# Attention gate in seven-product pairs, with the gated outputs' low parts on GpSimd, in a hybrid decoder layer

## The chip, the cores and the metric

One core of a Trainium2 chip runs the whole layer in one launch. The metric is the device time of that launch in microseconds (us). A change of about 0.2% (2.2 us) is what a measurement of this kernel can tell from none.

## The reference

`x` is 1 x 1024 x 1024 in fp32. Cut to what matters here:

```python
h = rmsnorm(x, ln_pre)
c_val, c_glu, c_gate, q, k, v, a_gate, g_conv, g_attn = split_columns(h @ w_in)
u  = c_val * sigmoid(c_glu)
c  = causal_depthwise_conv(u, w_dw, 31 taps) + b_dw
ya = silu(layernorm(c, ln_g, ln_b)) @ w_pw
ya = (ya * silu(c_gate)) @ w_br_conv
yb = sliding_window_attention(q, k, v, sinks)       # 16 query heads, 2 K/V heads, window 128
yb = (yb * silu(a_gate)) @ w_br_attn
m  = sigmoid(g_conv) * ya + sigmoid(g_attn) * yb
x  = x + rmsnorm(m @ w_out, ln_post)
x  = x + sigmoid(x @ w_ple_gate) * (p @ w_ple_proj)
```

`h @ w_in` makes, among others, the 1024 columns of `a_gate`, which this change is about.

## The kernel before

Activations lie channels by tokens: 8 tiles (KT) of 128 channels, 1024 tokens in two halves of 512. Every fp32 product is made of three TensorE passes in the fp32r format: each operand is split into a high part (ScalarE rounds it) and a low part (raw minus high, on VectorE or GpSimd), and hi*hi, lo*hi, hi*lo are added in PSUM. A matmul has 128 rows, 128 columns and 512 tokens.

Two kinds of product occur. A **plain tile** makes one tile of 128 output channels: 8 k-tiles x 3 passes x 2 halves = 48 matmuls (`tile`, `pairs`, `product`, L757). A **seven-product pair** makes two output tiles i and i+4 by Strassen-Winograd's scheme on 2 x 2 blocks: seven products of 4 k-tiles x 3 passes = 12 matmuls, 84 together instead of 96 (`early_product`, L944). It needs sums of weight blocks (`early_sum`, GpSimd, L1259), high and low parts of seven weight blocks (ScalarE L1437, GpSimd L1243, a ring of six slots in `pair_w`), copies of three products (`early_keep`, ScalarE L1451), and two subtractions (`early_take`, VectorE L2136).

The program's stages in order:

1. Start: `p @ w_ple_proj`, norm of x, two plain tiles each of GLU and value.
2. **Early stage**: the list `EARLY` has 18 pairs s = 0 to 17: GLU, value and conv gate (10), queries (3), swish gate of the conv branch CGATE (4), K/V (1, the last). Products run in `ORDER` P1, Q5, P6, P2, P7, Q3, P4. ScalarE prepares the high part of product b+6 behind the events of product b (`early_high`, `early_events`). VectorE runs the 31-tap convolution here, in `taps` between the products; the last of its eight rows ends in pair 17. GpSimd adds six finished rows into `sums` (`add_to_mean`), for the LayerNorm's mean.
3. Two plain query tiles (Q0), with K, V and rotary work beside them.
4. **Attention**: 16 steps p (8 blocks of 128 queries x 2 K/V groups). In each, TensorE makes `scores(p)`, `outputs(p-2)`, `turn(p-1)` (transposed probabilities) and 24 matmuls of a plain gate tile of g_attn (L1093). VectorE does `maxima`, `with_sinks`, `mask_turned(p-1)`, every second step one weight low part (`tile_low`), and `normalise`. ScalarE does `gate_half`, `copy_outputs`, `copy_turned`, the exponentials (`exps`) and weight high parts. GpSimd adds the last two rows into `sums`, then issues 16 DMAs of weight sums for later stages, each waiting for the one ahead of it (L1331, L1333).
5. **D0**: 8 plain tiles of a_gate. While they run, attention's last outputs are made, `conv_mean` and `wide_sums` (eight matmuls by `ones`) sum the statistics over channels, ScalarE applies silu to the gate, VectorE multiplies it into the attention outputs `qo`, both split the product (`split_high`, `split_low` into `o_hi`, `o_lo`), and VectorE and ScalarE make the LayerNorm statistics (`centre`, `square_conv`, `add_to_variance`, `root_step`, up to the semaphore `ln_root`).
6. **E0**: 8 plain tiles of `w_br_attn` on `o_hi`, `o_lo`, with scaling, silu and splitting of the convolution's rows beside them.
7. The two conv-branch products in seven-product pairs, then `w_out` and `w_ple_gate` in plain tiles.

The order on each engine is the order of the code; semaphores alone hold engines together. PSUM tensor `psg` holds the products in banks, `psb` the convolution's accumulators, then scores, then sums over channels.

## Time and profile before

| | us |
|---|---|
| median of 3 runs (1099.11 to 1099.71) | 1099.31 |
| the profiled execution's own time | 1099.16 |
| its span | 1097.4 |
| TensorE busy | 1090.2 (99%) |
| VectorE / ScalarE / GpSimd busy | 853.8 / 479.6 / 315.4 |
| attention, 441.7 to 583.8 | 142.1 |
| D0 with attention's end, 583.8 to 677.0 | 93.2 |
| E0, 677.0 to 764.0 | 87.0 |

Positions are us from the span's start. The chain of work that ended last is TensorE for 92% of the span; L757 and L944 have 33% and 30%. A matmul's duration (389 ns) contains its pipeline; what a further matmul costs is the distance between starts. VectorE's busy share by slices is 9 tenths over most of the early stage and 6 to 9 in attention; GpSimd's is 7 to 9 in the early stage, 5 and 2 in the two slices after it, and 0 beyond.

### The profile page before, as it was taken

The numbers are of one execution on the slowest core, as the hardware profiler recorded it, in microseconds if no ns is written. First come the engines' busy times: TensorE is split into PE (matmuls) and PEld (weight loads), VectorE is DVE, ScalarE is ACT, GpSimd is POOL, SyncE is SP. The second block draws the span as 40 slices with busy tenths as digits, with TensorE's granted clock in tenths as the row PEclk, the third lists the DMA queues.
The fourth block names the chain that finished last, engine by engine and source line by source line (L and its number), as shares of the span: only waits on it lengthen the run. The fifth ranks groups of instructions, "written<-read, shape, count | busy, mean of one in ns | idle before, by whom it ended". The sixth has DMA issues, their size and how long they took to land.

```text
span 1097.4 us, 16190 instructions
## 1 busy us (share of the span) xinstructions
PE 1090.2 (99%) x5992; PEld 886.1 (81%) x5992; DVE 853.8 (78%) x1201; ACT 479.6 (44%) x914; POOL 315.4 (29%) x252
## 2 busy tenths in 40 slices
PE   9999999999999999999999999999999999999998
PEld 7888888888888887777777888888888888888887
DVE  5998989989998986888874876466668778366776
ACT  6643343443334432665664433334436426344332
POOL 1069888887779852200000000000000000000000
PEclk9999999999999999999999999999999999999999
DMA  9802231422233348567751112354644843334655
GB/s 347 353 1 79 77 116 43 153 77 77 87 134 116 116 152 239 155 177 209 193 156 58 58 39 77 115 202 144 194 142 152 298 153 103 98 127 134 202 181 191
DMA packets 52822, 157.01 MB, mean 143 GB/s; under 512 B 6296, under 2 KB 7064, under 8 KB 50424
## 3 DMA queue, kind: packets, MB, share of 16 engines
q1 hardware_dynamic: 37232, 96.44, 25.8%
q10 hardware_dynamic: 13216, 42.87, 11.4%
q0 software_dynamic: 2304, 16.78, 6.2%
q8 instruction: 43, 0.70, 0.2%
q14 instruction: 27, 0.22, 0.1%
HBM read 124.90 MB, written 47.02 MB: 157 GB/s over the span
## 4 chain that ended last, share of the span: by engine, by line
PE 92%; DVE 3%; DMA 2%; ACT 1%; issue 1%; SPq 1%; POOL 0%; ACTq 0%; DVEq 0%
PE psg L757 33%; PE psg L944 30%; PE psb L1185 11%; PE psg L1093 7%; PE psg L781 2%; PE psb L1007 1%; PE psg L1064 1%; PE psg L1185 1%; DMA x_rows<-x_rows 1%; PE psg L810 1%; PE psg L1138 1%; PE psg L1025 1%; PE psg L1059 1%; ACT probs L1569 1%; DMA pack<-rotary 1%
## 5 line engine op out<-in xcount | busy, mean ns | idle before, releaser
L1243 POOL TENSOR_TENSOR pair_w<-early_raw,pair_w 128x512 fp32r<-128x512 f32 x117 | 157.5, 1356 | 79.4 <-ACT pair_w L1437 79.3
L944 PE MATMUL psg<-early_hi,pair_w 128*128 128x512 f32 x576 | 177.6, 389 | 0.2
L2098 DVE SCALAR_TENSOR_TENSOR psb<-conv,cols,psb 128x510 f32<-128x510 f32 (+6 forms) x196 | 137.1, 739 | 0.0
L944 PE MATMUL psg<-h_hi,pair_w 128*128 128x512 f32 x432 | 133.1, 389 | 1.3 <-DVE ring L2136 1.3
L944 PEld LDWEIGHTS psg<-early_hi,pair_w 128*128 128x128 f32 x576 | 107.9, 188 | 23.6 <-issue 1.4
L1437 ACT ACTIVATE pair_w<-early_raw 128x512 fp32r<-128x512 f32 x117 | 71.1, 626 | 117.4 <-POOL early_raw L1259 84.8
L1226 POOL TENSOR_TENSOR rstd<-mean_sq,expo 128x4 f32<-128x4 f32 x3 | 3.1, 1022 | 382.7 <-DVE mean_sq L1901 363.5
L944 PE MATMUL psg<-early_lo,pair_w 128*128 128x512 f32 x288 | 112.0, 389 | 0.0
L1887 DVE TENSOR_TENSOR w_lo<-w_raw,w_hi 128x1024 fp32r<-128x1024 f32 x57 | 69.8, 1224 | 41.0 <-ACT w_hi L1350 35.7
L944 PEld LDWEIGHTS psg<-h_hi,pair_w 128*128 128x128 f32 x432 | 81.0, 188 | 18.4 <-issue 1.7
L2098 DVE SCALAR_TENSOR_TENSOR psb<-fir_sum,fir_taps,psb 128x511 f32<-128x511 f32 (+14 forms) x120 | 88.8, 740 | 0.0
L1350 ACT ACTIVATE w_hi<-w_raw 128x1024 fp32r<-128x1024 f32 x58 | 61.2, 1055 | 53.9 <-PE psg L757 49.0
L944 PE MATMUL psg<-h_lo,pair_w 128*128 128x512 f32 x216 | 84.0, 389 | 0.0
L1259 POOL TENSOR_TENSOR early_raw<-early_raw 128x512 f32<-128x512 f32 x54 | 72.8, 1348 | 4.2
L1185 PE MATMUL psb<-s_hi,pair_w 128*128 128x512 f32 x240 | 73.9, 389 | 0.0
L944 PEld LDWEIGHTS psg<-early_lo,pair_w 128*128 128x128 f32 x288 | 54.1, 188 | 11.3
L757 PE MATMUL psg<-h_hi,w_hi 128*128 128x512 f32 x192 | 59.6, 391 | 0.0
L757 PE MATMUL psg<-h_hi,w_lo 128*128 128x512 f32 x192 | 59.2, 389 | 0.0
L757 PE MATMUL psg<-h_lo,w_hi 128*128 128x512 f32 x192 | 59.1, 389 | 0.0
L1680 ACT ACTIVATE pair_w<-block_raw 128x512 fp32r<-128x512 f32 x56 | 34.5, 626 | 41.8 <-PE psb L1185 21.5
L1185 PEld LDWEIGHTS psb<-s_hi,pair_w 128*128 128x128 f32 x240 | 45.1, 188 | 9.4
L1093 PE MATMUL psg<-h_hi,w_hi 128*128 128x512 f32 x128 | 51.8, 405 | 0.0
(344 smaller groups left out, 2467.9 us busy)
## 6 DMA issues: line engine op xcount, KB each, us to landing
w_raw<-weights SPq DMA_DIRECT2D x60, 512.0 KB, 3.3
gates<-ring ACTq DMA_DIRECT2D x30, 512.0 KB, 3.2
w_sums<-w_pairs POOLq DMA_DIRECT2D x12, 1024.0 KB, 8.0
ring<-gates ACTq DMA_DIRECT2D x24, 512.0 KB, 4.0
early_raw<-w_pairs SPq DMA_DIRECT2D x9, 1024.0 KB, 5.3
block_raw<-w_sums SPq DMA_DIRECT2D x32, 256.0 KB, 2.7
early_raw<-w_pairs SPq DMA_DIRECT2D x9, 768.0 KB, 4.4
block_raw<-w_pairs SPq DMA_DIRECT2D x24, 256.0 KB, 3.2
```

Source lines behind the costliest of these rows:

```text
L757: mm = nc.tensor.matmul(psg[:, slot, h * HALF:(h + 1) * HALF], w[:, wslot, (wk + k) * P:(wk + k + 1) * P], r[:, k, h * HALF:(h + 1) * HALF ...
L781: mm = nc.tensor.matmul(psg[:, slot, h * HALF:(h + 1) * HALF], w[:, slot, k * P:(k + 1) * P], r[:, k, h * HALF:(h + 1) * HALF], start=(k = ...
L944: mm = nc.tensor.matmul(bank, pair_w[:, at_w, w, k * P:(k + 1) * P], r[:, k, :], start=(not onto and k == 0 and m == 0), stop=(k == KP - 1 ...
L1093: mm = nc.tensor.matmul(gate_bank(p), w[:, t % 2, k * P:(k + 1) * P], r[:, k, half], start=(k == 0 and m == 0), stop=(k == KT - 1 and m == 2))
L1185: mm = nc.tensor.matmul(bank, pair_w[:, at_w, w, k * P:(k + 1) * P], r[:, k, :], start=(not onto and k == 0 and m == 0), stop=(k == KP - 1 ...
L1243: nc.gpsimd.tensor_tensor(pair_w[:, at_w, 1, :], early_source(s, n), pair_w[:, at_w, 0, :].bitcast(F32), ALU.subtract).then_inc(early_spli ...
L1259: nc.gpsimd.tensor_tensor(early_block(s, out), early_block(s, a), early_block(s, b), ALU.add).then_inc(early_summed, 1)
L1350: nc.scalar.activation(w_hi[:, j % 2, :], w_raw[:, j % 2, :], ACT.Copy).then_inc(w_hi_ready, 1)
L1437: nc.scalar.activation(pair_w[:, early_slot(b), 0, :], early_source(s, n), ACT.Copy).then_inc(early_split_hi, 1)
L1680: nc.scalar.activation(pair_w[:, pair_slot(b), 0, :], block_raw[:, b % 7, :], ACT.Copy).then_inc(pair_hi, 1)
L1887: nc.vector.tensor_tensor(w_lo[:, slot, :], w_raw[:, slot, :], w_hi[:, slot, :].bitcast(F32), ALU.subtract).then_inc(w_lo_ready, 1)
L2098: own.step(stt(acc[:, shift:], source[:, 0:HALF - shift], weight, acc[:, shift:], ALU.mult, ALU.add))
```

## The change

- The four pairs of a_gate (`AGATE`, silu) enter `EARLY` between CGATE and K/V, which becomes pair 21. The D0 tiles are gone; E0 is now tile 14. AGATE's results are written to DRAM in rows of 128 tokens (`AGATES`), 1024 pieces of 512 bytes a DMA where the other spills have 128 pieces of 4 KB, and are read back in attention block by block (`load_agate`).
- The LayerNorm statistics move from D0 into pairs 18 to 20 (`STATS` = 18): `mean_half`, `centre`, `square_conv` (now into PSUM banks 2 and 3), `add_to_variance`, `variance_half`, `first_root`, `last_root`, with the eight matmuls by `ones` ahead of products named in `WIDE`. `ln_root` is raised in pair 21. Centred rows go to DRAM (`CONV`) and come back into another buffer (`conv_norm`) by GpSimd DMAs once attention's buffers are free.
- The attention outputs are gated on VectorE within attention (`gate_outputs(p-3)`), split high on ScalarE (`o_high(p-4)`) and low on GpSimd (`o_low`), where `split_low` was on VectorE.
- TensorE goes from attention right into E0, whose first two tiles are made token half by token half, with attention's last outputs between.
- In the K/V pair the rotary work of VectorE (`rope`) now stands behind `early_take` 1.

```diff
+EARLY += [(AGATE, i) for i in range(PAIRS)] + [(KV, 0)]
+EARLY_MEANS = {4: 0, 6: 1, 8: 2, 11: 3, 13: 4, 15: 5, 17: 6}
+STATS = len(EARLY) - 4
+WIDE = {(STATS, P2): (1, 0), (STATS, Q3): (2, 1), (STATS + 2, P6): (3, 0), (STATS + 2, P7): (4, 1)}
+SQUARED = {(STATS, P4): 0, (STATS + 1, P1): 1, (STATS + 1, Q5): 2, (STATS + 1, P6): 3, (STATS + 1, P2): 4,
+           (STATS + 1, P7): 5, (STATS + 1, Q3): 6, (STATS + 1, P4): 7}
...
             for s in range(len(EARLY)):
                 for n in ORDER:
+                    if (s, n) in WIDE:
+                        wide_half(*WIDE[s, n])
                     early_product(s, n)
...
-            tile(D0 // 2, 0, h_hi, h_lo, beside=attention_end)
-            pe.wait_ge(o_ready, 2 * NB)
-            tile(D0 // 2, 1, h_hi, h_lo, beside=conv_mean)
-            pairs(D0 + 2, D0 + 4, h_hi, h_lo)
...
-            pairs(D0 + 6, E0, h_hi, h_lo)
-            pairs(E0, H0 - 2, o_hi, o_lo, KT)
+            for h in range(2):
+                pe.wait_ge(o_split_lo, NB * (h + 1))
+                for j in range(2):
...
+                    for k in range(KT):
+                        attention_end(h, j, k)
...
+            pairs(E0 + 2, H0 - 2, o_hi, o_lo)
...
             low(C0)
-            pool.wait_ge(last_roped, 1)
-            add_to_mean(KT - 2)
-            add_to_mean(KT - 1)
             made = 0
...
+            def o_low(p):
+
+                pool.wait_ge(o_split_hi, p + 1)
+                nc.gpsimd.tensor_tensor(o_block(o_lo, p), o_block(qo, p), o_block(o_hi, p).bitcast(F32),
+                                        ALU.subtract).then_inc(o_split_lo, 1)
+
+            for p in range(LAST_P - 3):
+                o_low(p)
+            pool.wait_ge(conv_spilled, 16 * KT)
+            conv_rows(0)
+            for p in range(LAST_P - 3, 2 * NB):
+                o_low(p)
+            pool.wait_ge(conv_back, 16 * PAIRS)
+            conv_rows(1)
...
+            def square_conv(c):
+
+                act.wait_ge(centred, c + 1)
+                if c:
+                    act.wait_ge(var_summed, c)
+                nc.scalar.activation(banks23, conv[:, c, :], ACT.Square).then_inc(sq_made, 1)
...
+                if p > 3:
+                    o_high(p - 4)
...
+            def centre(c):
+
+                dve.wait_ge(mean_done, 2)
+                stt(conv[:, c, :], banks01, -1.0 / D, conv[:, c, :], ALU.mult, ALU.add).then_inc(centred, 1)
+
+            def add_to_variance(c):
+
+                dve.wait_ge(sq_made, c + 1)
...
+                if (s, n) in SQUARED:
+                    c = SQUARED[s, n]
+                    centre(c)
+                    if c:
+                        add_to_variance(c - 1)
+                if (s, n) == (STATS + 2, P1):
+                    add_to_variance(KT - 1)
+                    variance_half(0)
...
+            def gate_outputs(p):
...
+                nc.vector.tensor_tensor(o_block(qo, p), o_block(qo, p), agate[n % 2][:, 4 * g:4 * g + 4, :], ALU.mult).then_inc(o_gated, 1)
...
                 with_sinks(p)
+                if p > 2:
+                    gate_outputs(p - 3)
```

How the instructions stand now, at three places (line numbers are those of each kernel's own file).

ScalarE at the end of a swish-gate pair, before: the events of P2 and P4 (reads of the product into `ring`), the two spills, and between them the high parts `pair_w`.

```order
L1467 ACTIVATE ring<-psg 128x512
L1437 ACTIVATE pair_w<-early_raw 128x512
L1467 ACTIVATE ring<-ring 128x512 x2
L1467 ACTIVATE ring<-psg 128x512
L1364 DMA gates<-ring 128x1024 x2
L1437 ACTIVATE pair_w<-early_raw 128x512
L1451 ACTIVATE psg<-psg 128x512
```

ScalarE at the end of pair 19, after; `psb<-conv` is `square_conv`, here of rows 4 to 7:

```order
L1552 ACTIVATE psb<-conv 128x1024
L1497 ACTIVATE pair_w<-early_raw 128x512
L1552 ACTIVATE psb<-conv 128x1024
L1497 ACTIVATE pair_w<-early_raw 128x512
L1552 ACTIVATE psb<-conv 128x1024
L1497 ACTIVATE pair_w<-early_raw 128x512
L1527 ACTIVATE ring<-ring 128x512 x2
L1527 ACTIVATE ring<-psg 128x512
L1539 DMA agate<-ring 1024x1x128 x2
L1552 ACTIVATE psb<-conv 128x1024
L1497 ACTIVATE pair_w<-early_raw 128x512
L1511 ACTIVATE psg<-psg 128x512
```

Four squares of 1024 elements stand in the same stretch, the last one behind the spills of pair 19.

VectorE where the statistics were, in D0, before; `conv<-psb,conv` is `centre`, `sums<-sums,ring` is `add_to_variance`:

```order
L2340 TENSOR_TENSOR qo<-qo,tanh_t 128x1024
L1887 TENSOR_TENSOR w_lo<-w_raw,w_hi 128x1024
L2316 SCALAR_TENSOR_TENSOR conv<-psb,conv 128x1024 x2
L1896 SCALAR_TENSOR_TENSOR o_lo<-qo,o_hi 128x1024
L2322 TENSOR_TENSOR sums<-sums,ring 128x1024 x2
L2340 TENSOR_TENSOR qo<-qo,tanh_t 128x1024
L1887 TENSOR_TENSOR w_lo<-w_raw,w_hi 128x1024
L2316 SCALAR_TENSOR_TENSOR conv<-psb,conv 128x1024 x2
L1896 SCALAR_TENSOR_TENSOR o_lo<-qo,o_hi 128x1024
```

VectorE in pair 19 from P7 on, and the head of pair 20, after; `ring<-kept_q_121,psg` and `ring<-psg,kept` are `early_take` 1 and 2:

```order
L2261 TENSOR_TENSOR sums<-sums,psb 128x1024
L2212 TENSOR_TENSOR ring<-kept_q_121,psg 128x512
L2252 SCALAR_TENSOR_TENSOR conv<-psb,conv 128x1024
L2261 TENSOR_TENSOR sums<-sums,psb 128x1024
L2212 TENSOR_TENSOR ring<-psg,kept 128x512
L2252 SCALAR_TENSOR_TENSOR conv<-psb,conv 128x1024
L2261 TENSOR_TENSOR sums<-sums,psb 128x1024
L2252 SCALAR_TENSOR_TENSOR conv<-psb,conv 128x1024
L2261 TENSOR_TENSOR sums<-sums,psb 128x1024 x2
L1981 CAST post_hi<-sums 128x512
L1983 TENSOR_TENSOR sums_lo<-sums,post_hi 128x512
L1981 CAST post_hi<-sums 128x512
```

Each `centre` and `add_to_variance` now has its place between products of a pair; the two takes, which wait for P7 and Q3, stand ahead of three of them.

GpSimd behind the early stage, before:

```order
L1236 TENSOR_TENSOR w_lo<-w_raw,w_hi 128x1024
L1236 TENSOR_TENSOR w_lo<-w_second,w_hi 128x1024
L1236 TENSOR_TENSOR w_lo<-w_raw,w_hi 128x1024
L1265 TENSOR_TENSOR sums<-sums,conv 128x1024 x2
L1331 DMA w_sums<-w_pairs 128x2048
L1333 DMA w_sums<-w_pairs 128x2048
L1331 DMA w_sums<-w_sums 128x2048
L1333 DMA w_sums<-w_pairs 128x2048
L1331 DMA w_sums<-w_sums 128x2048
```

GpSimd there, after, at the chain's start:

```order
L1273 TENSOR_TENSOR w_lo<-w_raw,w_hi 128x1024
L1273 TENSOR_TENSOR w_lo<-w_second,w_hi 128x1024
L1273 TENSOR_TENSOR w_lo<-w_raw,w_hi 128x1024
L1367 DMA w_sums<-w_pairs 128x2048
L1369 DMA w_sums<-w_pairs 128x2048
```

And at the chain's end, 12 DMAs later, still GpSimd, after:

```order
L1367 DMA w_sums<-w_pairs 128x2048
L1369 DMA w_sums<-w_pairs 128x2048
L1386 TENSOR_TENSOR o_lo<-qo,o_hi 128x4x128 x12
L1381 DMA conv_norm<-conv 128x1024 x4
L1386 TENSOR_TENSOR o_lo<-qo,o_hi 128x4x128 x4
L1381 DMA conv_norm<-conv 128x1024 x4
```

The two 1024-wide additions ahead of the chain of DMAs are gone; behind its last DMA stand twelve low parts in a row, four loads, and four more low parts.

## Rows read from the trace of the kernel before

**Rows 1.** Page, part 1: TensorE's busy time, share of the span, instructions.

```profile
PE 1090.2 (99%) x5992; PEld 886.1 (81%) x5992; DVE 853.8 (78%) x1201; ACT 479.6 (44%) x914; POOL 315.4 (29%) x252
```

**Rows 2.** Windows by stage: busy us and count of each engine, granted clock, DMA.

```profile
73.70:400.00 326.30, 326.07 (x1437) 269.16 (x1436) 299.18 (x446) 129.72 (x225) 267.06 (x210) 1.00 0.26 91
...
441.70:583.80 142.10, 141.70 (x1761) 104.54 (x1761) 116.92 (x247) 89.73 (x342) 15.11 (x18) 1.00 0.63 172
583.80:677.00 93.20, 93.20 (x440) 75.12 (x439) 61.38 (x55) 34.88 (x36) 0.95 (x1) 1.00 0.17 56
```

**Rows 3.** Waits of TensorE: us in total, times, longest.

```profile
PE psg L944 <- DVE ring L2136: 1.3, 1, 1.3
...
PE psb L1007 <- ACT probs L1569: 0.3, 1, 0.3
```

**Rows 4.** TensorE's timeline, first pair stage: start, us, engine, line, names, shape.

```profile
73.67 0.62 PE L944 MATMUL psg<-h_hi,pair_w 128*128 128x512 f32 x2
...
74.35 0.62 PE L944 MATMUL psg<-h_hi,pair_w 128*128 128x512 f32 x2
```

**Rows 5.** Timeline in the K/V pair: start, us, engine, line, operation, names, shapes.

```profile
412.26 3.09 DVE L2157 TENSOR_TENSOR rtmp<-rtmp,sin_t 96x1024 f32<-96x1024 f32 x1
```

**Rows 6.** ScalarE's timeline where a swish-gate pair stage ends.

```profile
379.50 0.60 ACT L1467 ACTIVATE ring<-psg 128x512 f32<-128x512 f32 x1 [1.04 <-PE psg L944]
380.13 0.81 ACTq L1364 DMA_DIRECT2D gates<-ring  x2
```

**Rows 7.** Issue times of one SyncE queue line of 512 pieces (ns).

```profile
L634 SPq DMA_DIRECT2D early_raw<-w_pairs x9: 551/552/1070, 35.8 to 347.6; - x9
```

**Rows 8.** Page, part 6: the spills of early pairs: KB each, us to landing.

```profile
gates<-ring ACTq DMA_DIRECT2D x30, 512.0 KB, 3.2
```

**Rows 9.** VectorE's and ScalarE's timelines of the old LayerNorm statistics (604 us, then 605).

```profile
604.31 2.35 DVE L2316 SCALAR_TENSOR_TENSOR conv<-psb,conv 128x1024 f32<-128x1024 f32 x2
...
607.71 2.55 DVE L2322 TENSOR_TENSOR sums<-sums,ring 128x1024 f32<-128x1024 f32 x2
...
605.57 2.19 ACT L1640 ACTIVATE ring<-conv 128x1024 f32<-128x1024 f32 x2 [1.15 <-DVE conv L2316]
```

**Rows 10.** GpSimd's timeline, from the last weight tile to the last weight-sum DMA.

```profile
433.73 2.40 POOL L1236 TENSOR_TENSOR w_lo<-w_raw,w_hi 128x1024 fp32r<-128x1024 f32 x1 [10.59 <-ACT w_hi L1350]
...
445.78 0.79 POOL L1331 DMA_DIRECT2D w_sums<-w_pairs  x1
...
555.87 0.81 POOL L1333 DMA_DIRECT2D w_sums<-w_pairs  x1 [4.66 <-DMA w_sums<-w_pairs]
```

**Rows 11.** VectorE line 2143: operand in PSUM, then both in SBUF (ns min/median/max).

```profile
L2143 DVE SCALAR_TENSOR_TENSOR conv<-ring,psg x6: 673/680/689, 103.8 to 264.9; 128x512 f32<-128x512 f32 x6
L2143 DVE SCALAR_TENSOR_TENSOR conv<-ring,conv x6: 1642/1722/1803, 107.2 to 262.5; 128x512 f32<-128x512 f32 x6
```

**Rows 12.** GpSimd line 1243, 128x512 low parts (ns min/median/max).

```profile
L1243 POOL TENSOR_TENSOR pair_w<-early_raw,pair_w x117: 1294/1307/3422, 64.6 to 410.6; 128x512 fp32r<-128x512 f32 x117
```

**Rows 13.** VectorE's timeline: line 2233 beside a GpSimd addition, and with GpSimd idle.

```profile
445.25 0.62 DVE L2233 SCALAR_TENSOR_TENSOR smax<-smax,sinks 128x8 f32<-128x8 f32 x1
...
569.28 0.17 DVE L2233 SCALAR_TENSOR_TENSOR smax<-smax,sinks 128x8 f32<-128x8 f32 x1
```

**Rows 14.** Timeline of one attention step, all engines.

```profile
565.07 1.29 DVE L2251 TENSOR_TENSOR probs<-probs,rden 128x512 f32<-128x512 f32 x2
...
568.47 0.71 PE L1025 MATMUL psg<-ident,probs 64*128 64x64 f32 x16
...
569.69 0.17 DVE L2237 TENSOR_TENSOR esink<-sinks,smax 128x8 f32<-128x8 f32 x1
...
570.41 1.40 DVE L2262 TENSOR_TENSOR pt_prev<-pt_all,mixed 64x512 f32<-64x512 f32 x2 [0.55 <-ACT pt_all L1555]
```

**Rows 15.** Timeline where attention ends.

```profile
593.43 0.66 PE L1059 MATMUL psg<-pt_prev,vstep 64*64 64x256 f32 x8
...
595.15 0.60 ACT L1582 ACTIVATE qo<-psg 128x512 f32<-128x512 f32 x1 [4.83 <-PE psg L1064]
```

More of the change, by code:

```diff
@@ L53 @@
 C0 = 6
-D0 = 14
-E0 = 22
-H0 = 30
-I0 = 46
-TILES = 62
-WTILES = 46
+E0 = 14
+H0 = 22
+I0 = 38
+TILES = 54
+WTILES = 38
 PAIRS = KT // 2
@@ L637, in _ @@
                     sp.dma_start(early_rest[:], WPAIR[:, 3, s, :]).then_inc(early_loaded[1], 16)
+                if s == len(EARLY) - 1:
+                    for c in range(KT):
+                        sp.wait_ge(centred, c + 1)
+                        sp.dma_start(CONV[:, c, :], conv[:, c, :]).then_inc(conv_spilled, 16)
             def load_tile(t):
@@ L761, in product, with wide_half @@
                 mm.then_inc(tile_done, 1)
+            def wide_half(count, h):
+                pe.wait_ge(parts_ready, count)
+                for part, source in enumerate((post_hi[:], sums_lo[:, h * HALF:(h + 1) * HALF])):
+                    mm = nc.tensor.matmul(psb[:, h, :], ones[:], source, start=(part == 0), stop=(part == 1))
+                mm.then_inc(mean_done, 1)
             def first_pair():
@@ L1098, in _, with attention_end, merge_bank @@
                 attention(p)
[L1100 to L1101 removed]
+            def attention_end(h, j, k):
+                if (h, j, k) == (0, 0, 2):
                     outputs(LAST_P - 1)
[L1103 removed]
+                elif (h, j, k) == (0, 0, 4):
                     turn(LAST_P)
[L1105 removed]
+                elif (h, j, k) == (0, 1, 2):
                     outputs(LAST_P)
[L1108 to L1118 removed]
+            def merge_bank(j, h):
+                return psb[:, h, :] if j else psg[:, 0, h * HALF:(h + 1) * HALF]
             pe.wait_ge(half_free, NB)
@@ L1477, in early_spill @@
                     act.wait_ge(early_tanh, READ_BASE[s] + READS[s])
+                if kind == AGATE:
+                    act.dma_start(AGATES[:, :, i + KP * row, :], blocks_of(ring[:, row, :])).then_inc(spilled[row], 16)
+                    return
                 spill(GATES[:, i + KP * row + KT * {CGATE: 1, GCONV: 2, QUERY: 3}[kind], :], row)
@@ new lines, in variance_half, with first_root @@
+            def variance_half(h):
+                dve.wait_ge(var_summed, KT)
+                if h:
+                    dve.wait_ge(mean_done, 3)
+                sums_in_parts(post_hi[:], (upper, lower)[h])
+            def first_root(half, bank):
+                dve.wait_ge(mean_done, 4)
+                own.step(nc.vector.tensor_scalar(sums[:, half], banks01[:, half], 1.0 / D, EPS, ALU.mult, ALU.add))
+                own.wait()
+                own.step(nc.vector.tensor_scalar(root[:].bitcast(I32), sums[:, half].bitcast(I32), -0.5, ROOT_SEED,
+                                                 ALU.mult, ALU.add))
+                own.wait()
+                root_step(half, root[:], psb[:, bank, :])
@@ new lines, in last_root, with statistics @@
+            def last_root(half, bank):
+                root_step(half, root[:], psb[:, bank, :])
+                step = psb[:, bank, :]
+                own.step(nc.vector.tensor_tensor(step, root[:], root[:], ALU.mult))
+                own.wait()
+                own.step(stt(step, step, -0.5, sums[:, half], ALU.mult, ALU.mult))
+                own.wait()
+                own.step(stt(sums[:, half], step, 1.5, root[:], ALU.add, ALU.mult))
+                own.wait()
+            def statistics(s, n):
+                if (s, n) == (STATS, P1):
+                    mean_half(0)
+                if (s, n) == (STATS, P2):
+                    mean_half(1)
+                if (s, n) in SQUARED:
+                    c = SQUARED[s, n]
[5 more added lines that the diff above has]
+                    variance_half(0)
+                if (s, n) == (STATS + 2, P6):
+                    variance_half(1)
+                if (s, n) == (STATS + 2, P7):
+                    first_root(upper, 2)
+                if (s, n) == (STATS + 2, Q3):
+                    last_root(upper, 2)
+                if (s, n) == (STATS + 2, P4):
+                    first_root(lower, 3)
+                if (s, n) == (STATS + 3, P1):
+                    last_root(lower, 3)
+                    dve.nop(nofuse=True).then_inc(ln_root, 1)
@@ L2184, in _ @@
                     taps((VAL_TAPS if kind == VAL else OTHER_TAPS)[n])
+                    statistics(s, n)
             def rope_in_place(j, columns, before, kept=None, rotated=None):
@@ new lines, in _, with norm_scale, c_low @@
+            gate_outputs(LAST_P - 1)
+            mask_turned(LAST_P, 0)
+            mask_turned(LAST_P, 1)
+            gate_outputs(LAST_P)
+            def norm_scale(c):
+                k = NORM[c]
+                dve.wait_ge(conv_back, 16 * (PAIRS if c < PAIRS else KT))
+                nc.vector.tensor_tensor(conv_norm[:, k, :], conv_norm[:, k, :], sums[:], ALU.mult).then_inc(ln_scaled, 1)
+            def c_low(c):
+                k = NORM[c]
+                dve.wait_ge(hi_ready, c + (KT + 1))
+                blocks, row, src = ((0, k, conv_norm[:, k, 0:HALF]) if k < KP else
+                                    (slice(1, 3), k - KP, conv_norm[:, k, :].rearrange("p (h s) -> p h s", h=2)))
```

259 lines of the change are left out of this document (124 added, 135 removed).

## The prediction

> **What bounds the kernel now.** I read the page's busy shares first [rows 1]: TensorE is busy 99% of the span, so time goes away only where TensorE gets fewer matmuls, and comes back only where it is made to wait. The windows by stage [rows 2] say that this holds in every stage the change touches: 326.07 of 326.30 us in the early pairs, 141.70 of 142.10 in attention, 93.20 of 93.20 in D0. They also show who is nearly full beside it: VectorE 299 of 326 us and GpSimd 267 of 326 in the early pairs, VectorE 117 of 142 in attention, while in D0 GpSimd is idle and VectorE at two thirds. Then the waits of TensorE [rows 3]: of those in these stages only two matter, 1.3 us for a `ring` read of VectorE in the K/V pair, and 0.3 us for an exponential in the third step of attention. Last the distance of matmuls [rows 4]: three start in 74.35 - 73.67 = 0.68 us, 0.2267 each. A product of twelve is 2.72 us, a pair of 84 is 19.04, a plain pair of 96 is 21.76.
>
> **What is removed.** Eight plain tiles, 8 x 48 = 384 matmuls, become four pairs, 4 x 84 = 336. The eight matmuls by `ones` are moved, not added. So 48 x 0.2267 = **-10.9 us**, on the path, since TensorE has no gap there. The clock granted is full in all windows [rows 2].
>
> **K/V pair.** The 1.3 us wait [rows 3] is P4 waiting for `early_take` 1, which stood behind the first rotary operations, one of them at 3.09 us [rows 5]. The take now goes first, and its successor is wanted only by the transposes of V four us into the next tile. **-1.3 us**. The 0.3 us wait at attention's third step lies at the end of a chain through VectorE that began with line 2233 at 0.62 us under a GpSimd addition, against 0.17 later [rows 13]; that addition is gone. **-0.3 us**.
>
> **Early pairs 17 to 20.** The last convolution row, GpSimd's two 1024-wide additions and `mean_half` come a half to a whole pair ahead of the `ones` matmuls: nothing. But the statistics are a chain between VectorE and ScalarE, one link per product: a centring (2.35/2 = 1.2), a square (2.19/2 = 1.1), an addition (2.55/2 = 1.3) [rows 9]. Until P2 of pair 19 the links fit into 2.72 us. At P7 VectorE must first wait for that product (take 1), and ScalarE's square 5 waits behind it. From the end of P7 I add up: take 0.7 (an operand in PSUM, [rows 11]), centre 5 1.2, addition 4 1.3, square 5 1.1, addition 5 1.3, square 6 1.1, a weight high part and three swishes, each 0.6 [rows 6] and together 2.3, the two spills, square 7 1.1, addition 7 1.3, and cast and subtraction for `variance_half`, 0.7 each at most [rows 11], 1.3. Without the spills that is 12.7. The spills took 0.81 for two with 128 pieces each [rows 6]; now a spill has 1024. The nearest row is an issue of 512 pieces at 0.55 us [rows 7]; from 0.4 for 128 to 0.55 for 512 the line goes on to about 0.8 for 1024, so 1.6 for two. Sum 14.3 us. TensorE wants the result at P6 of pair 20, four products or 10.9 us behind P7. Wait: **+3.4**, and with a few hundredths for each of a dozen semaphores **+4.0**. Bounds: 0 if squares run ahead of what I think, 2.6 with spills at 0.81, 5.3 if GpSimd's operation (1.3, [rows 12]) stands in the way of the subtraction, which has both operands in SBUF. ScalarE's `keep` of P1, which P6 also needs, lies 1 us ahead of this and is covered by it.
>
> On that subtraction and on the next term: an operation of VectorE takes 0.68 us with one operand in PSUM, and 1.72 with both in SBUF while GpSimd works [rows 11], six times in six. So it waits 1.04 on average for an operation of 1.3 [rows 12]. The Trainium skill (SBUF — State Buffer, "Who interferes with whom") gives this as an exclusive lock that the first to start holds for its whole instruction, and lets casts in the two-port mode take it as well. No row here shows a cast blocked; by the page the cast ahead of the subtraction would wait too, another 1.3 us at most for the wait of pair 20.
>
> **Attention.** Each step gets a gating multiplication on VectorE (0.7, both operands in SBUF) from p = 3, a high part on ScalarE (0.6) from p = 4, a load issue every second step, and a low part on GpSimd (1.3). What hides them is slack at `turn`: the normalised probabilities of step 14 end at 566.4 and the turn that reads them starts at 568.5 [rows 14], 2.1 us; VectorE also idles about 1.3 us a step. One each of 0.7, 0.6 and a wait of 1.0 fits in: nothing in a steady step.
>
> It isn't steady. GpSimd's queue holds the 16 weight-sum DMAs ahead of the low parts. Before, they ran from 445.8 to 556.7 [rows 10]; now they start when the last weight tile ends at 436.1, so end near 547. `o_low` 0 to 7 are by then ready, 8 comes at once: nine operations of 1.3 back to back. In step 12 VectorE has eight operations with both operands in SBUF from `smax` to the second half of the probabilities (smax, esink, gate, two masks, denominator, two halves), and takes turns with GpSimd. At least seven wait, 1.04 to 1.3 each [rows 11, 12]: 7.3 to 9.1, plus 0.7 for the gate, less 1.3 idle and 2.1 slack: 4.6 to 6.4 us later at `turn`. ScalarE's exponentials run beside some of it. I take **+4.7**. Bounds: 0 if VectorE gets in between, 8 if the burst reaches into a second step.
>
> **Attention's end.** D0 hid the last outputs. Now E0's second half needs `o_low` 15. In the old trace outputs(15) starts at 593.4 and its copy at 595.15 [rows 15]; E0 sets outputs(15) after the same 30 matmuls, so at about the same place. Behind the copy (0.6) come gate 0.7, high 0.6, low 1.3 and hops: ready near 598.9. TensorE has 18 matmuls behind outputs(15), to 599.2. That just fits; but masks of step 15 and the first row scalings share the lock with four low parts. **+0.6**, bounds 0 and 3. If the cover were gone wholly it would be 3.9 us. GpSimd's four loads, 0.8 us of issue each [rows 10], stand ahead of low parts 12 to 15 and are over by then. E0's `norm_scale` waits for loads that have 10 us of room.
>
> **Sum** against the profiled execution: -10.9 - 1.3 - 0.3 + 4.0 + 4.7 + 0.6 = -3.2, from 1099.16 to 1096.0 (span 1097.4 to 1094.2); the median was 0.15 above it, so **1096.2 us**.
>
> **The rivals.**
>
> *Only the pair-20 wait.* Speaks for it: VectorE's order in attention leaves holes for two GpSimd operations under the PSUM maxima, and if the DMA chain ends later or in a hole, fewer collide. Then 0.5 for 4.7: 1092.0.
>
> *Only the lock in attention.* The chain of squares could be shorter than my sum, as ScalarE may issue spills quicker. 1092.2.
>
> *Neither.* The matmuls alone, with 0 to 1 for the end: 1087.0 to 1088.0. Against it: VectorE is near full where the work goes, and rows 11 leave no doubt on the wait itself.
>
> *Slower: the spills of the attention gate.* The place is `ring` after pairs 17 to 20. A spill landed in 3.2 us in 128 pieces [rows 8]; with 1024 it costs the same if bytes count and up to 8 x 3.2 = 25.6 if pieces count. ScalarE reads P2 of the next pair into that row 10.9 us into the pair, some 2 us behind the issue; so beyond 9 us ScalarE, and all high parts and keeps behind it, stand still, and P7, which needs `keep` of P6, follows with a little slack. Each us above 9 costs nearly 4; at 12 us the change is 8 us slower than my forecast, 1104, at 25 over 1130. It decides from about 11 us.
>
> **How the numbers follow.** Both waits 0.42, own range 1093.5 to 1099; the pair-20 wait alone 0.18; the lock alone 0.12; neither 0.13; spills, or a burst that comes back in further steps, 0.15. The range 1088.5 to 1100.0 leaves out half of "neither" and most of the last. A measurement here tells 0.2%, 2.2 us, from no change: faster is under 1097.1. Of the first case about two thirds lie there, with the next three 0.70; the same 0.18; slower 0.12.
>
> **What would show it.** 336 more matmuls on the line of `early_product` and 384 fewer on `tile`'s. A wait of TensorE for VectorE's `sums_lo` at P6 of pair 20 of about 4 us; if it is absent or doubled, that term is wrong. The K/V wait gone. In attention one step, near the end of the `w_sums` DMAs, longer by 4 to 5 us, TensorE waiting for `probs`, with masks and probabilities at 1.7 for 0.7; all other steps as long as before. At the end a wait for `o_lo` under 1 us. Spills that land above 9 us, or ScalarE waiting for them, would make the forecast wrong altogether; so would any wait of TensorE behind E0 that was not there.

## The result: 1109.0 us, 9.7 us slower where 3.1 us faster was forecast

| | before | changed |
|---|---|---|
| median of 5 executions, us | 1099.31 (1098.48 to 1099.71) | 1108.99 (1106.00 to 1111.39) |
| the profiled execution's own time, us | 1099.16 | 1111.39 |
| its span, us | 1097.4 | 1109.6 |

The ratio is 1.0089, 95% interval 1.0078 to 1.01. The forecast was 1096.2, its range 1088.5 to 1100.0; the sign was wrong too. The changed kernel scatters over 5.4 us where the kernel before scatters over 1.2 here; in the larger groups below, single executions of the kernel before reached 1104.1 us too. The profiled execution is the slowest of the five.

The page's busy line of the changed kernel has 48 matmuls fewer than [rows 1], as the change says:

```profile
PE 1086.3 (98%) x5944; PEld 881.0 (79%) x5944; DVE 865.9 (78%) x1217; ACT 494.2 (45%) x961; POOL 398.2 (36%) x319
```

The waits of TensorE (us in total, times, longest), which answer to [rows 3]. The first three are 17.3 us; the forecast had 4.0 and 4.7 for two of them and none for the third:

```profile
PE psb L1046 <- ACT probs L1641: 8.5, 1, 8.5
PE psb L797 <- DVE sums_lo L1983: 4.5, 1, 4.5
PE psg L981 <- DVE ring L2212: 4.3, 1, 4.3
```

The chain of work that ended last (start, us, engine, what), followed back over the two places. The first piece is pairs 19 to 21, the second attention's step 12:

```profile
461.84 1.04 ACT psb L1552
462.90 1.23 DVE sums L2261
464.15 0.91 DVE post_hi L1981
465.09 1.66 DVE sums_lo L1983
466.79 1.22 PE psb L797 x2
...
484.11 0.61 ACT ring L1527
484.74 0.54 ACTq L1539
485.31 18.50 DMA agate<-ring
503.89 0.70 DVE ring L2212
504.72 5.24 PE psg L981 x12
...
641.73 11.72 DVE smax L2383
653.88 1.11 ACT probs L1641 x6
655.53 2.63 PE psb L1046 x64
```

Read downwards: the last square, the last addition, a cast and a subtraction, and only then the `ones` matmuls of pair 20. Then the second spill of the last gate pair, which took 18.5 us to land, and the take that had to wait for its `ring` row. Then `smax`, an operation on 8 elements per partition, which took 11.7 us where its siblings take 0.17 [rows 13].

Behind each of the three waits TensorE got the lower of its two clocks. Windows of the changed kernel (length, TensorE busy, its count, granted clock, DMA):

```profile
466.80:472.00 5.20, 5.20 (x12) 0.50 0.00 0
472.00:478.00 6.00, 6.00 (x27) 1.00 0.01 3
504.70:509.60 4.90, 4.88 (x12) 0.50 0.45 176
655.50:659.80 4.30, 4.27 (x76) 0.50 0.80 241
659.80:665.00 5.20, 5.20 (x41) 1.00 0.02 7
```

A clock of 0.50 is 1.2 GHz, 1.00 is 2.4. Twelve matmuls took 5.2 and 4.9 us where 12 x 0.2267 [rows 4] is 2.7, so 2.5 and 2.2 us were lost beyond the waits, and up to 2.1 in the third window. Before, it was full in the three stages of [rows 2].

The sum of what the profile shows, against the profiled execution of before: -10.9 for the matmuls; pair 20 +4.5 and +2.5 of clock; K/V pair +3.0 (4.3 in place of 1.3) and +2.2; step 12 +8.5 and up to +2.1; step 3 -0.3. Together +11.6, and 1111.39 - 1099.16 is +12.2. Nothing of size is missing.

### The profile page after: what moved, and what is told of

Read it like the earlier page. It is cut to its first block, busy times and chain, and to the rows that moved or that the text cites. A ratio compares the mean times of both kernels' runs of the same rounds, so it can differ in the third digit from the quotient of the medians.

```text
span 1109.6 us, 16292 instructions
## 1 busy us (share of the span) xinstructions
PE 1086.3 (98%) x5944; PEld 881.0 (79%) x5944; DVE 865.9 (78%) x1217; ACT 494.2 (45%) x961; POOL 398.2 (36%) x319
## 4 chain that ended last, share of the span: by engine, by line
PE 88%; DVE 5%; DMA 4%; ACT 2%; issue 1%; ACTq 0%; SPq 0%; DVEq 0%
PE psg L981 36%; PE psg L787 23%; PE psb L1222 11%; PE psg L1132 6%; PE psg L818 2%; DMA agate<-ring 2%; PE psb L1046 1%; DMA conv<-xT 1%; PE psg L1222 1%; PE psg L1103 1%; DVE smax L2383 1%; ACT probs L1641 1%; PE psg L1163 1%; PE psb L1163 1%; PE psg L847 1%; PE psg L1175 1%
## 5 line engine op out<-in xcount | busy, mean ns | idle before, releaser
L1280 POOL TENSOR_TENSOR pair_w<-early_raw,pair_w 128x512 fp32r<-128x512 f32 x143 | 192.8, 1358 | 95.9 <-ACT pair_w L1497 95.9
L981 PE MATMUL psg<-early_hi,pair_w 128*128 128x512 f32 x704 | 218.6, 392 | 0.2
L981 PE MATMUL psg<-h_hi,pair_w 128*128 128x512 f32 x528 | 164.5, 393 | 4.3 <-DVE ring L2212 4.3
L981 PEld LDWEIGHTS psg<-early_hi,pair_w 128*128 128x128 f32 x704 | 133.1, 189 | 29.1 <-issue 1.4
L981 PE MATMUL psg<-early_lo,pair_w 128*128 128x512 f32 x352 | 137.8, 392 | 0.0
L981 PEld LDWEIGHTS psg<-h_hi,pair_w 128*128 128x128 f32 x528 | 100.1, 190 | 25.5 <-issue 4.7
L981 PE MATMUL psg<-h_lo,pair_w 128*128 128x512 f32 x264 | 103.5, 392 | 0.0
L981 PEld LDWEIGHTS psg<-h_lo,pair_w 128*128 128x128 f32 x264 | 50.2, 190 | 10.5
L1132 PE MATMUL psg<-h_hi,w_hi 128*128 128x512 f32 x128 | 51.9, 405 | 0.0
L2504 DVE TENSOR_TENSOR pair_w<-block_raw,pair_w 128x512 fp32r<-128x512 f32 x56 | 37.9, 685 | 17.4 <-ACT pair_w L1757 17.4
```

What stands on the lines that cost most here:

```text
L981: mm = nc.tensor.matmul(bank, pair_w[:, at_w, w, k * P:(k + 1) * P], r[:, k, :], start=(not onto and k == 0 and m == 0), stop=(k == KP - 1 ...
L1132: mm = nc.tensor.matmul(gate_bank(p), w[:, t % 2, k * P:(k + 1) * P], r[:, k, half], start=(k == 0 and m == 0), stop=(k == KT - 1 and m == 2))
L1280: nc.gpsimd.tensor_tensor(pair_w[:, at_w, 1, :], early_source(s, n), pair_w[:, at_w, 0, :].bitcast(F32), ALU.subtract).then_inc(early_spli ...
L2504: nc.vector.tensor_tensor(pair_w[:, at_w, 1, :], block_raw[:, b % 7, :], pair_w[:, at_w, 0, :].bitcast(F32), ALU.subtract).then_inc(pair_l ...
```

## What VectorE met in step 12

The timeline of step 12 (start, us, engine, line, operation, names, shapes):

```profile
641.49 0.81 POOL L1369 DMA_DIRECT2D w_sums<-w_pairs  x1 [5.01 <-DMA w_sums<-w_pairs]
...
641.73 11.71 DVE L2383 SCALAR_TENSOR_TENSOR smax<-smax,sinks 128x8 f32<-128x8 f32 x1
...
642.05 11.35 POOL L1386 TENSOR_TENSOR o_lo<-qo,o_hi 128x512 fp32r<-128x512 f32 x9
...
655.53 2.63 PE L1046 MATMUL psb<-kdup,qo 64*32 64x160 f32 x64 [8.54 <-ACT probs L1641]
```

The last weight-sum DMA is issued, nine low parts follow without a gap (11.35 / 9 = 1.26 each), and VectorE stands still for all nine. The forecast had the place, the step and the count right, and supposed turns: one low part, one operation of VectorE, and so on. That is what rows 11 had shown. Two questions followed: whether the row, and not something else in the step, cost the time; and what makes VectorE lose nine turns where it had never lost two.

## Experiments

The runs came in three groups, each on one chip with the kernel before beside it (medians 1099.95, 1100.08 and 1100.10). Ratios are to that kernel; differences between altered kernels of different groups, and to the 1109.0 above, rest on these medians being alike.

### Low parts that wait for one another

```diff
                 pool.wait_ge(o_split_hi, p + 1)
+                if p:
+                    pool.wait_ge(o_split_lo, p)
```

> Each of GpSimd's low parts waits, beside its high part, for the low part ahead of it, so that it is never ready while that one runs; nothing else changes, the nine still stand one behind the other. Theory A, that GpSimd keeps the port between two operations when the second is ready as the first begins, and gives it up otherwise: VectorE's smax operation of that step takes at most 1.5 us in place of 11.71, VectorE and GpSimd take turns from there, TensorE's wait for the exponentials falls from 8.5 to 1 to 4.6 us, and the whole takes 1098 to 1104 us. Theory B, that nine operations in a row shut VectorE out whatever stands between them: smax stays at 11 to 12 us and the whole at 1106 to 1111 us.

Measured: 1101.14 us (1098.55 to 1103.61), ratio to before 1.0011 (1.0 to 1.0023). The longest `smax` was 1.08 us, TensorE's waits in attention 4.1 us in all. A wait that adds nothing but a wait gave back 5 to 8 us. Theory A's numbers all came. But in this profile the row of low parts began while VectorE was inside a `w_lo` of 1.23 us, not ahead of `smax`; and another kernel below, without the added wait, took turns as well. So this run shows that the row was the cost, and not yet why it shut VectorE out.

### Low parts between the DMAs, and on VectorE

```diff
+LOW_BEHIND = (7, 9, 10, 11, 12, 13, 14, 16)
...
+                    if made + 1 in LOW_BEHIND:
+                        o_low(next(lows))
```

> The first eight low parts stand between GpSimd's DMAs of weight sums, one each behind the 7th, 9th, 10th to 14th and 16th, where their high parts should just be ready (high parts come every 8.9 us, the DMAs every 7.65). If the row of nine is what costs, TensorE's wait of 8.5 us and the stretch at a lower granted clock behind it (0.79 and 0.66) go: 10 to 12 us less, 1096 to 1099 us; the longest smax is under 1.6 us. Rival, that GpSimd's DMA issue in front of the row held VectorE and not the row itself: now single stalls of over 2 us stand beside several of the DMAs, and the whole stays above 1103 us.

Measured: 1097.17 us (1095.31 to 1098.91), ratio 0.9974 (0.9962 to 0.9985). The longest `smax` was 1.25 us; TensorE waited 2.9 us in four pieces for probabilities. So the row of nine is the cost. But the rival's sign came in part: beside three of the DMAs an operation of VectorE of 0.7 us took 2.05, 2.34 and 3.38 us. The first two came up between an issue and its low part and lasted to that low part's end and their own time. The third is the first half of the probabilities, at the one DMA with two low parts behind it; it came up 0.04 us ahead of them and stayed out for both:

```profile
641.38 0.81 POOL L1379 DMA_DIRECT2D w_sums<-w_pairs  x1 [5.54 <-DMA w_sums<-w_pairs]
...
641.89 3.99 DVE L2407 TENSOR_TENSOR probs<-probs,rden 128x512 f32<-128x512 f32 x2
641.93 2.78 POOL L1363 TENSOR_TENSOR o_lo<-qo,o_hi 128x512 fp32r<-128x512 f32 x2
```

The whole is still far below the 1103 us that the rival asked for.

```diff
-            for p in range(LAST_P - 3):
-                o_low(p)
...
+                if p > 4:
+                    o_low(p - 5)        # now an operation of VectorE
```

> The low parts go back to VectorE, one step behind their high parts (0.7 us each); GpSimd has none. Theory, that only the row on GpSimd hurt and VectorE has 1.3 us a step to spare: 1096 to 1099 us, no wait of TensorE for the exponentials. Rival, that VectorE is full in attention with the gating in it: steps 5 to 15 become 0.3 to 0.6 us longer each, 3 to 6 us in all, 1100 to 1104 us.

Measured: 1094.86 us (1094.15 to 1095.04), ratio 0.9952 (0.9935 to 0.9968). Sixteen low parts of 0.685 us, no wait of TensorE for probabilities. VectorE had the room. So the move of the low parts to GpSimd is what cost most, 12 to 14 us of the changed kernel's 1106.7 (below) to 1109.0, by the medians: with them on VectorE, the rest of the change gains 5.1 us over the kernel before. The profiled executions are 16.5 us apart (1111.39 and 1094.93), of which up to 10.6 stand in step 12 and 6.5 at the K/V wait with its clock, which the second profile does not have and which the low parts, made later, do not cause.

### The last sums over channels one product later

```diff
-(STATS + 2, P6): (3, 0), (STATS + 2, P7): (4, 1)}
+(STATS + 2, P7): (3, 0), (STATS + 2, Q3): (4, 1)}
```

> The last four matmuls by ones stand one product later: ahead of P7 and Q3 of pair 20 in place of P6 and P7, two products behind P6 for the first. The wait of 4.5 us for sums_lo goes to under 0.3 us, and with it the stretch at a lower granted clock behind it (0.85 over 451.5 to 475): 5.5 to 7 us less than the changed kernel, 1102 to 1103.5 us. Rival, that the roots behind it then come too late for pair 21 and the wait only moves: 1105 us or more, with a new wait at Q3 or behind.

Measured: 1101.19 us (1095.01 to 1103.87), ratio 1.0002 (0.9983 to 1.0021); the wait for `sums_lo` is gone, two of 1.8 and 1.1 us stand in the pairs behind, and the median is just under the range expected. Its profile held the surprise. Eleven low parts in a row, with no added wait, and VectorE in between all the same:

```profile
642.44 0.81 POOL L1369 DMA_DIRECT2D w_sums<-w_pairs  x1 [7.95 <-DMA w_sums<-w_pairs]
643.00 15.97 POOL L1386 TENSOR_TENSOR o_lo<-qo,o_hi 128x512 fp32r<-128x512 f32 x11
...
650.95 0.98 DVE L2383 SCALAR_TENSOR_TENSOR smax<-smax,sinks 128x8 f32<-128x8 f32 x1
651.97 1.22 DVE L2385 TENSOR_SCALAR nmax<-smax 128x8 f32<-128x8 f32 x1
653.22 1.21 DVE L2387 TENSOR_TENSOR esink<-sinks,smax 128x8 f32<-128x8 f32 x1
```

Three small operations, one low part of waiting each: the turns of the forecast. Readiness alone does not shut VectorE out, so Theory A as written for the first experiment falls.

### The changed kernel once more

> The changed kernel once more, unaltered. With the K/V pair's spill left to chance (it landed in 18.5 us in the profile of the changed kernel, in 13.2 to 15.2 us in four others of the same pair), its time should spread over several us. If GpSimd's row shuts VectorE out every time in this kernel, all executions lie at 1106 to 1111.5 us and the profile shows an operation of VectorE at over 5 us. If the shut-out hangs on how row and VectorE happen to meet, some lie at 1098 to 1102 us.

Measured: 1106.74 us (1101.64 to 1110.31). Its profiled execution was the one of 1101.64, and there the same program took turns:

```profile
647.65 0.81 POOL L1369 DMA_DIRECT2D w_sums<-w_pairs  x1 [8.48 <-DMA w_sums<-w_pairs]
648.21 15.82 POOL L1386 TENSOR_TENSOR o_lo<-qo,o_hi 128x512 fp32r<-128x512 f32 x11
...
656.03 0.96 DVE L2383 SCALAR_TENSOR_TENSOR smax<-smax,sinks 128x8 f32<-128x8 f32 x1
```

Two profiles of one program differ in when the 16th DMA lands: in one VectorE came up with `smax` 0.24 us behind the next issue, in the other it was already inside `w_lo`. That may be part of the scatter (two profiles do not show how often each happens), and gave the theory for the next run. Turns are not cheap either: TensorE waited 0.6, 1.3, 0.6 and 1.6 us, and the clock fell behind these short waits too (windows with the columns as above):

```profile
660.00:665.00 5.00, 1.66 (x68) 0.88 0.53 133
665.00:670.00 5.00, 5.00 (x35) 0.50 0.20 80
```

The K/V pair had no wait of TensorE in this profile.

### Rows set up at chosen places

```diff
+KICK = {6: ('smax', 1), 9: ('reduce', 1), 12: ('smax', 1), 15: ('smax', 0)}
...
+                pool.wait_ge(o_split_hi, 3 * n + 3)
+                pool.wait_ge(ang_ready, n + 2)      # raised by VectorE at the place named
+                if KICK[p][1]:
+                    next(sums_of)                   # issues one DMA
+                for low in range(3 * n, 3 * n + 3):
+                    o_low(low)
```

> GpSimd's first twelve low parts in four rows of three, in steps 6, 9, 12 and 15, each started by VectorE: in steps 6 and 12 the start is given right ahead of smax and GpSimd first issues a DMA of weight sums, as stood ahead of the row of nine; in step 9 the same with the start ahead of the last maximum, 0.7 us earlier; in step 15 ahead of smax and with no DMA. Theory, that a VectorE operation that comes up while GpSimd issues a DMA with ready low parts behind it stays shut out for the whole row: in steps 6 and 12 one VectorE operation takes 3 to 4 us, in step 15 none takes over 2.6. Rival, that any row met at its head by a small operation shuts it out: step 15 too has one at 3 to 4 us. Second rival, turn-taking everywhere: none over 2 us (two operations of GpSimd's 1.3 at most). The four last weight-sum DMAs come late here, and TensorE may wait for low parts at attention's end, so the time of the whole, some 1100 to 1110 us, says nothing.

Measured: the high part, not the start given by VectorE, turned out to come last, so the rows began beside the mask operations and not at `smax`. In steps 6 and 12 a mask operation began within a hundredth of a microsecond of the DMA issue, and the two masks took 2.40 us. In step 15, with no DMA, they took 3.34, which is turns. In step 9 the mask came up 0.30 us behind the issue and 0.24 ahead of the row, and two masks took 5.29 us, where two take 1.40: the row's 3.8 us and their own time. So the shut-out came back, at the one place of the four with that order of events, though not where it was meant. (1128.57 us in all: TensorE waited 25.6 us for late low parts at attention's end, as this kernel puts the DMAs ahead of them.)

### The same state four times, with and without readiness, with and without the DMA

```diff
+            for p, lows in ((7, range(0, 3)), (9, range(3, 6)), (11, range(6, 8)), (13, range(8, 10))):
+                next(sums_of)                       # waits for the DMA ahead
+                pool.wait_ge(o_split_hi, p - 3)
+                next(sums_of)                       # issues one DMA
+                for low in lows:
+                    o_low(low, low > lows[0])
```

> The state of step 9 in the kernel with four rows, set up four times: in steps 7, 9, 11 and 13 GpSimd waits for the high part of that step, issues one DMA of weight sums and has ready low parts behind it (3, 3, 2 and 2). VectorE's first mask operation should come up some 0.3 us behind the DMA's start. Theory: each time that it does, the mask operation takes the whole row and its own 0.7, 4.5 us with three low parts and 3.2 with two. Rival, chance: one or none is over 2 us. The last weight-sum DMAs come late, so the time of the whole is not to be read.

> The same, but within a row each low part also waits for the one ahead of it, so it is not ready while that one runs; the start of a row is unaltered. Theory, that the shut-out lasts only as long as the next operation is ready: the mask operation takes at most 2 us each time (one low part and its own 0.7). Rival: once shut out, VectorE stays so to the end of the row, 3.2 to 4.5 us as without the waits.

> The same rows in the same steps with the DMA behind the row in place of ahead of it. Theory, that the shut-out begins only when VectorE comes up between a DMA issue and the row behind it: the mask operation comes up while the first low part runs, and the two take turns, under 2.1 us for one operation. Rival, that any row whose members are ready shuts out: 3.2 to 4.5 us again.

In step 9 the first two kernels met in the same state: `smax` came up 0.14 us behind the start of the issue, the row 0.44 us behind `smax`. First the kernel whose low parts are ready:

```profile
610.01 0.82 POOL L1374 DMA_DIRECT2D w_sums<-w_pairs  x1 [13.27 <-ACT o_hi L1685]
610.15 4.49 DVE L2400 SCALAR_TENSOR_TENSOR smax<-smax,sinks 128x8 f32<-128x8 f32 x1
610.59 4.01 POOL L1392 TENSOR_TENSOR o_lo<-qo,o_hi 128x512 fp32r<-128x512 f32 x3
```

Then the one whose low parts wait for each other; VectorE gets its turn after the first:

```profile
608.84 0.82 POOL L1374 DMA_DIRECT2D w_sums<-w_pairs  x1 [13.28 <-ACT o_hi L1687]
608.98 2.03 DVE L2402 SCALAR_TENSOR_TENSOR smax<-smax,sinks 128x8 f32<-128x8 f32 x1
609.42 4.72 POOL L1394 TENSOR_TENSOR o_lo<-qo,o_hi 128x512 fp32r<-128x512 f32 x3
...
611.25 1.17 DVE L2406 TENSOR_TENSOR esink<-sinks,smax 128x8 f32<-128x8 f32 x1
```

And with the DMA behind the row, `smax` coming up inside the first low part:

```profile
607.91 3.80 POOL L1392 TENSOR_TENSOR o_lo<-qo,o_hi 128x512 fp32r<-128x512 f32 x3 [13.51 <-issue]
608.44 0.78 DVE L2400 SCALAR_TENSOR_TENSOR smax<-smax,sinks 128x8 f32<-128x8 f32 x1
609.26 1.23 DVE L2402 TENSOR_SCALAR nmax<-smax 128x8 f32<-128x8 f32 x1
610.52 1.21 DVE L2404 TENSOR_TENSOR esink<-sinks,smax 128x8 f32<-128x8 f32 x1
```

The other steps: in the first kernel step 13 shut the second mask operation out for a row of two (4.12 us for both masks; the second came up some 0.5 us behind the issue, just ahead of the row), while in steps 7 and 11 the mask had begun beside the issue and took turns (2.42 and 2.45). In the second kernel step 11 had the mask 0.28 us behind the issue and took turns (3.85 for two, the GpSimd row stretched by 0.5). In the third no operation waited for more than one low part. The state came less often than expected. But all five times that VectorE came up between an issue and a ready row (the changed kernel, step 9 of the kernel with chosen places, steps 9 and 13 of the first one here, and the two low parts of the kernel with low parts between the DMAs) it was shut out for the whole row, nine, three, three, two and two low parts long; and both times that the members of the row waited for each other (steps 9 and 11 of the second) it had its turn after the first. That order of events is not the only one that does it, as the last kernel below shows. The times of the whole were measured once each: 1101.65, 1098.33 and 1096.40 us.

### Two and three parts together

> Low parts on VectorE and the four last matmuls by ones one product later. If the two costs are independent, the gains add: 1094.9 with the low parts alone, less the pair-20 wait of 4.5 and 1.5 to 2 us of lower clock behind it: 1088 to 1089.5 us. Rival, that the K/V wait grows by what pair 20 gives back, since the spill then has less time: 1091 to 1093 us, with a wait for the spill of 3 us or more.

Measured: 1090.37 us (1089.65 to 1093.13), ratio 0.991 (0.9893 to 0.9926). That is 4.5 under the low parts on VectorE alone, less than the 6 to 6.5 expected, and above the range given. In the profiled execution, the slowest of four, VectorE did not wait for a spill, so the rival's sign is absent, but a longer wait, of 2.7 us, stood at attention's first scores, for a rotary operation of VectorE (line 2343; 0.7 with the low parts on VectorE alone).

```diff
-                    act.dma_start(AGATES[:, :, i + KP * row, :], blocks_of(ring[:, row, :])).then_inc(spilled[row], 16)
+                    spill(AGATES[:, i + KP * row, :], row)
...
-                act.dma_start(agate[n % 2][:], AGATES[:, n, :, :]).then_inc(agate_loaded, 16)
+                act.dma_start(agate[n % 2][:], AGATES[:, :, n * P:(n + 1) * P]).then_inc(agate_loaded, 16)
```

> The same, and the gate's spills written in 128 pieces of 4 KB in place of 1024 of 512 bytes; the blocks are cut out when they are loaded in attention, 1024 pieces a load as before. If small pieces are what makes the last spill slow beside SyncE's loads, it lands in 5 to 8 us, VectorE's wait for it goes, and the whole takes 1 to 3 us less than with two changes alone: 1086.5 to 1088 us. Rival, that the queues' load alone (a DMA share of 0.8 to 1.0 there) makes it slow: landing stays at 13 us or more and the time does not change.

Measured: 1087.66 us (1087.30 to 1087.97), ratio 0.9887 (0.9871 to 0.9904): 12.4 us faster than the kernel before, with a scatter of 0.7 us. DMAs between 478 and 520 us of the kernel with 512-byte pieces (issuer, count, KB each, median us to landing):

```profile
agate<-ring ACTq DMA_DIRECT2D x2, 512.0 KB, 10.3
...
pack<-ring ACTq DMA_DIRECT2D x2, 64.0 KB, 6.1
```

and with 4 KB pieces, the same bytes:

```profile
agate<-ring ACTq DMA_DIRECT2D x2, 512.0 KB, 7.8
...
pack<-ring ACTq DMA_DIRECT2D x2, 64.0 KB, 3.3
```

The slowest spill went from 12.3 to 8.4 us, just above the 5 to 8 expected, and the copy of K to `pack`, on which the rotary work and then attention's first scores hang, from 6.1 to 3.3. VectorE's wait for that copy fell from 8.1 to 4.5 us and TensorE's wait at the first scores went. So in these two profiles the gain is there, and not at the wait for a spill that the expectation named. Piece size and load seem to act together: the quickest spill in small pieces landed in 3.6 us, in large ones in 2.7. No run took the load away. The Trainium skill (DMA: Bandwidth & Descriptors, "Queues, rings and completion order") says that a DMA engine serves its queues in turn, a whole packet from one before it goes to the next. The landings can be read that way; no run here shows the turns themselves.

> Low parts on GpSimd one by one between its DMAs, the four matmuls by ones one product later and the spills in 4 KB pieces: the fastest form with low parts on GpSimd. Beside the same with low parts on VectorE (1087.7) it should be slower by what the single low parts hold VectorE up, as with the other two parts unaltered (1097.2 to 1094.9): 1089 to 1090.5 us. Rival, that those 2.3 us came from a longer K/V wait in that kernel: 1087.5 to 1088.

Measured: 1092.14 us (1090.34 to 1094.06), ratio 0.9928 (0.9903 to 0.9952), 4.5 us slower than the same with low parts on VectorE, more than expected. TensorE waits 2.4 us in five pieces for probabilities and 0.8 for `w_lo`. So even one at a time the low parts cost more on GpSimd (1.3 us, and VectorE held) than on VectorE itself (0.7). This profile also has the one case that the order "issue, VectorE, row" does not cover. VectorE came up 0.31 us behind the start of two low parts, as the issue in front of them was just over, and stayed out for both, with an operation on 8 elements per partition:

```profile
635.37 0.81 POOL L1379 DMA_DIRECT2D w_sums<-w_pairs  x1 [5.55 <-DMA w_sums<-w_pairs]
635.93 2.78 POOL L1363 TENSOR_TENSOR o_lo<-qo,o_hi 128x512 fp32r<-128x512 f32 x2
...
636.24 2.50 DVE L2400 TENSOR_TENSOR denom<-denom,esink 128x8 f32<-128x8 f32 x1 [1.77 <-ACT esink L1652]
```

## The prediction, step by step

- **Matmuls, -10.9.** Right. With the three costs taken away the kernel takes 1087.66 us, inside the 1087.0 to 1088.0 that the rival "neither" gave for the matmuls alone.
- **K/V pair, -1.3.** Failed, at the sentence "The take now goes first". It does, but it also needs its `ring` row free, and that row held the last spill. Measured in the profile: +3.0 of wait, and 2.2 of clock behind it. The rival on spills had the mechanism, and this is the spill of pair 20, one of the four it named; but the one that waited was VectorE's take and not ScalarE, and a high piece count alone did not do it, as the eight spills landed in a median of 4.8 us. The rival did not look at what SyncE issues beside the last one: from 484 us `w_raw`, `w_second`, the tables, the rotary rows and `qo`, with a DMA share of 0.79 between 495 and 515. In the ten other profiles with small pieces this spill took 12.2 to 15.2 us, the take waited up to 3.4 us, and TensorE waited 1.1 us at most, in the second profile of the same program not at all. So this term varies from execution to execution, and mostly the 1.3 us did go.
- **Pair 20, +4.0.** Right for the wait: 4.5 us at the product named, through the chain named. The size came out partly by errors that cancel. Cast and subtraction took 0.91 and 1.65 us where 1.3 was put for both, as GpSimd worked beside them (that the subtraction would be held was the bound of 5.3); the spills took 1.25 us for two where the estimate was 1.6, and squares and additions were each up to a tenth shorter. The cast was held as well: 0.91 beside GpSimd, 0.42 in the kernel before at 1009 us with GpSimd idle. That is the sentence on casts of the Trainium skill's page (SBUF — State Buffer, "Who interferes with whom"), which the prediction could not take from a row; the trace agrees with it.
- **Attention, +4.7.** Place, count and step right, size wrong: 8.5 of wait and up to 2.1 of clock. The step that failed is "takes turns with GpSimd", taken from six cases of the early stage, where GpSimd issues no DMA [rows 11]. The bound "8 if the burst reaches into a second step" was the nearest end. Where turns are taken the wait was about right: the profile of 1101.64 us has 0.6, 1.3, 0.6 and 1.6 us there, 4.1 in all; but the clock behind them took up to 2.8 more. The rule of the Trainium skill (SBUF — State Buffer, "Who interferes with whom"), that the first to issue has the port pair for its whole instruction, speaks of one instruction; here the trace goes beyond it, with VectorE held through nine.
- **A term that was missing: the clock.** 2.5, 2.2 and up to 2.1 us, some 7 in all. The text said "the clock granted is full in all windows" and left it there, although it forecast waits of four microseconds in two places. A wait of TensorE was priced at its length alone. With it, the profile is off the forecast by 6.5 us at the K/V pair, 5.9 in attention and 3.0 at pair 20.
- **Step 3, -0.3, and attention's end, +0.6.** The wait at step 3 is gone. At the end no wait for `o_lo` is shown: the last low part began at 698.45 and took 1.54 us, the products that need it began at 700.53. The term was 0; its bounds held.

The forecast gave slower 0.12. What happened is both costs of the likeliest case, one of them doubled, and, in the slowest execution at least, the last spill of the slower rival with another engine waiting for it; and what all three have in common, the low clock behind a wait, was in no case.

## To carry to other kernels

Price a wait of TensorE with what follows it: here each wait of 4 to 9 us was followed by 4 to 5 us at half clock, 2 to 2.5 us more, and several waits of 1 to 2 us close together did the same. Before giving GpSimd a row of operations that all become ready behind one slow DMA, ask what VectorE does if it gets no turn until the row ends; spread them, make each wait for the one ahead, or leave them on VectorE if it has the room. And of a transfer that a buffer waits for, look at what the other queues issue in the same microseconds, and keep its pieces large.

## What the hardware showed beyond what was expected

- VectorE can be held for a whole row of GpSimd operations: 11.7 us for an operation of 0.17 us behind nine low parts, 4.5 behind three. It was seen six times, each with a DMA issue of GpSimd right ahead of the row and the row's members ready. Five times VectorE's operation came up 0.14 to 0.55 us behind the start of the issue and ahead of the row, once 0.31 us behind the start of the row. A semaphore wait between the members restored turns (2.03 us in the same state). Five rows without a DMA in front took turns, and so did rows with one where VectorE's next operation came up some 0.15 us behind the row's start. What opens the shut-out is not settled: without a DMA in front VectorE always came up after the row had begun, and no run shows what sets the sixth case apart.
- TensorE's granted clock stood at 0.50 for 5.2, 4.9 and 4.3 us behind waits of 4.5, 4.3 and 8.5 us, and was back at 1.00 after that. Shorter waits can do it too: behind a wait of 2.9 us (low parts that wait for one another) and one of 2.7 us (two parts together) it stood at 0.50 for over 3 us, and behind waits of 1.3, 0.6 and 1.6 us within 5 us (the changed kernel once more) for over 5. Behind a single wait of 1.3 us, in the kernel of 1087.66 us, it stayed at 1.00.
- A spill of 512 KB in 512-byte pieces landed in 3.5 us at best and in 18.5 at worst within one execution.
